# Sixteen projection tiles of the third layer: one product of 512 columns and one of 256 in place of three of 256

## The reference, cut to what matters

```python
h = rmsnorm(x, norm_mix_g)
proj = h @ w_in                 # query, key, value of an mLSTM; output gate; query, key, value of a
                                # dilated attention (1536 columns each); gates (2048)
q, k = q_a / sqrt(64), k_a      # 3 groups x 8 heads x 64
y_b = dilated attention(q, k, v_a)
y_a = mLSTM(...)
merged = sigmoid(g_a) * (y_a @ w_proj_a) + sigmoid(g_b) * (y_b @ w_proj_b)
x = x + merged @ w_out
```

## Time and profile before

| | |
|---|---|
| median of 3 runs | 1105.75 us |
| profiled execution | 1105.73 us |
| its span | 1103.6 us |
| TensorE busy | 1090.9 us, 99% |
| VectorE busy | 757.8 us, 69% |
| ScalarE busy | 600.3 us, 54% |
| GpSimd busy | 149.6 us, 14% |

### The profile page before, as it was taken

The page is one execution under the profiler, slowest core; times in us unless marked ns, Lnnn a source line. Parts: engine busy times, 40 slices in busy tenths (PEclk is TensorE's granted clock), DMA queues, the critical chain, the costliest instruction groups (busy, mean ns, idle before and its releaser), DMA issues.

```text
span 1103.6 us, 17798 instructions
## 1 busy us (share of the span) xinstructions
PE 1090.9 (99%) x6977; PEld 973.0 (88%) x6977; DVE 757.8 (69%) x1054; ACT 600.3 (54%) x788; POOL 149.6 (14%) x113
## 2 busy tenths in 40 slices
PE   8999999999999999999999999999999999999997
PEld 7868888888998888888889999898899989999997
DVE  6774665656668466656557878576587577988884
ACT  6574644444698464444455546555555357546454
POOL 4652000000377220000030000000000002000003
PEclk9999999999999999999999999999999999999999
DMA  9836565556433156565645654446653556545631
GB/s 303 289 117 123 188 223 191 191 190 233 138 106 129 33 161 217 187 195 189 200 154 191 191 158 144 131 153 231 201 166 121 168 214 229 200 176 196 226 136 39
DMA packets 138929, 194.00 MB, mean 176 GB/s; under 512 B 7163, under 2 KB 113112, under 8 KB 138860
## 3 DMA queue, kind: packets, MB, share of 16 engines
q1 hardware_dynamic: 129004, 184.02, 50.7%
q10 hardware_dynamic: 9248, 8.95, 3.2%
q0 software_dynamic: 608, 0.08, 0.1%
HBM read 191.90 MB, written 6.37 MB: 180 GB/s over the span
## 4 chain that ended last, share of the span: by engine, by line
PE 91%; ACT 4%; DVE 4%; issue 1%; DVEq 0%; ACTq 0%
PE psum L628 22%; PE psum L629 22%; PE psum L630 22%; PE psum L842 11%; PE psum L846 6%; ACT arena L1755 3%; PE psum L716 2%; PE psum L746 1%; PE psum L1392 1%; PE psum L1419 1%; DVE arena L2711 1%; DVE st L2710 1%; PE psum L1353 0%; PE psum L904 0%; PE psum L906 0%
## 5 line engine op out<-in xcount | busy, mean ns | idle before, releaser
L2417 DVE TENSOR_TENSOR wlo<-raw,whi 128x2048 fp32r<-128x2048 f32 (+1 forms) x134 | 302.4, 2264 | 134.8 <-ACT whi L1769 133.7
L1769 ACT ACTIVATE whi<-raw 128x2048 fp32r<-128x2048 f32 (+1 forms) x149 | 277.4, 1871 | 174.0 <-PE psum L630 126.3
L628 PE MATMUL psum<-xA,whi 128*128 128x256 f32 x840 | 239.2, 285 | 0.0
L630 PE MATMUL psum<-xA,wlo 128*128 128x256 f32 x840 | 237.6, 283 | 0.0
L629 PE MATMUL psum<-xA,whi 128*128 128x256 f32 x840 | 237.6, 283 | 0.0
L1726 POOL TENSOR_TENSOR wlo<-raw,whi 128x288 fp32r<-128x288 f32 (+3 forms) x43 | 81.8, 1930 | 746.5 <-ACT whi L1769 746.2
L628 PEld LDWEIGHTS psum<-xA,whi 128*128 128x128 f32 x840 | 160.3, 191 | 2.9 <-DVE wlo L2648 0.9
L629 PEld LDWEIGHTS psum<-xA,whi 128*128 128x128 f32 x840 | 160.4, 191 | 1.1
L630 PEld LDWEIGHTS psum<-xA,wlo 128*128 128x128 f32 x840 | 160.3, 191 | 0.1
L842 PE MATMUL psum<-xA,whi 128*128 128x512 f32 x512 | 122.5, 390 | 0.0
L628 PE MATMUL psum<-whi,xC 128*128 128x512 f32 (+1 forms) x296 | 114.5, 387 | 0.0
(11 more groups left out here) (311 smaller groups left out, 1685.7 us busy)
## 6 DMA issues: line engine op xcount, KB each, us to landing
raw<-in_w_in SPq DMA_DIRECT2D x42, 1024.0 KB, 5.0
raw<-in_mlp_w_up SPq DMA_DIRECT2D x32, 1024.0 KB, 5.3
raw<-in_mlp_w_down SPq DMA_DIRECT2D x32, 1024.0 KB, 4.8
raw<-in_w_gate SPq DMA_DIRECT2D x11, 1024.0 KB, 5.2
raw<-in_w_up SPq DMA_DIRECT2D x11, 1024.0 KB, 6.4
down_raw<-in_w_down SPq DMA_DIRECT2D x6, 1024.0 KB, 8.1
arena<-in_w_down SPq DMA_DIRECT2D x5, 1024.0 KB, 8.3
raw<-in_b_w_o SPq DMA_DIRECT2D x4, 1024.0 KB, 5.0
```

The costliest lines, as they stand in the source:

```text
L628: nc.tensor.matmul(out, lh, rh, start=start, stop=False, skip_group_check=skip)
L630: return nc.tensor.matmul(out, ll, rh, start=False, stop=stop, skip_group_check=skip)
L1769: nc.scalar.activation(whi[split_of[c]][:, 0:n], raw_bufs[raw_of[c]][:, 0:n], ACT.Copy).then_inc(hi_sem, 1)
L2417: V.tensor_tensor(wlo[split_of[c]][:, 0:n], raw_bufs[raw_of[c]][:, 0:n], f(whi[split_of[c]][:, 0:n]), ALU.subtract).then_inc(lo_sem["dve"], 1)
```

## The change

The sixteen tiles qa0 to qa5, ka0 to ka5 and pa0 to pa3 go through a new function `both_parts`. For each half of 128 features it uses a bank of its own: eight products of 512 columns (high weight by both input parts) give the sum with the high inputs in columns 0 to 255 and that with the low inputs in 256 to 511; eight products of 256 columns (low weight) are added to the former. A tile takes two neighbouring banks: qa4 4-5, qa5 6-7, ka0 4-5; qa0 6-7, qa1 4-5, qa2 6-7, qa3 4-5; ka1 6-7, ka2 4-5, ka3 6-7, ka4 4-5, ka5 6-7; pa0 2-3, pa1 4-5, pa2 6-7, pa3 2-3. ScalarE copies columns 256 to 511 of both banks into the tile (`half_copy`), VectorE adds columns 0 to 255 (`parts_added`, two operations), GpSimd multiplies the tile by the row of factors or the gate (`scale_tiles`). TensorE waits for GpSimd's results before the first logits, VectorE before the merge. The diff, without the lines of semaphore plans:

```diff
+            def both_parts(name, x, b):
+                c = index[name]
+                hi, lo = slot(c, KT, 256)
+                weights(c)
+                for nt in range(2):
+                    out = open_bank(f"{name}.{nt}", b + nt)
+                    for k in range(KT):
+                        nc.tensor.matmul(out, hi[:, k, nt * P:nt * P + P], x[:, :, k, :], start=k == 0, stop=False)
+                    for k in range(KT):
+                        ins = nc.tensor.matmul(out[:, 0:SEQ], lo[:, k, nt * P:nt * P + P], x[:, 0, k, :],
+                                               start=False, stop=k == KT - 1)
+                    close_bank(ins, f"{name}.{nt}")
+                chunk_done[c] = full[f"{name}.1"]
...
-            feature_major("qa4", xA, 4)
-            feature_major("qa5", xA, 5)
-            feature_major("ka0", xA, 6)
+            both_parts("qa4", xA, 4)
+            both_parts("qa5", xA, 6)
+            both_parts("ka0", xA, 4)
...
-                feature_major(f"qa{h}", xA, 4 + (h + 3) % 4)
+                both_parts(f"qa{h}", xA, (6, 4)[h % 2])
...
-                feature_major(f"ka{j}", xA, 4 + (j + 2) % 4)
+                both_parts(f"ka{j}", xA, (4, 6)[j % 2])
...
-                wait_read(f"qa{j}.0")
-                wait_read(f"ka{j}.0")
+                pe.wait_ge(*done[f"C.qa{j}"])
+                pe.wait_ge(*done[f"C.ka{j}"])
...
-                feature_major(f"pa{j}", xB, 2 + j % 2)
+                both_parts(f"pa{j}", xB, (2, 4, 6, 2)[j])
...
+            def scale_tiles():
+                pool.wait_ge(*read["C.rs"])
+                run(nc.gpsimd.tensor_scalar(query_row, row_scale, A_DIM ** -0.5, None, ALU.mult))
+                for name in tile_order:
+                    j, row = int(name[2]), query_row if name[0] == "q" else row_scale
+                    for nt in range(2):
+                        pool.wait_ge(*read[f"{name}.{nt}"])
+                    v = C[name[0:2]][:, 2 * j:2 * j + 2, :]
+                    run(T(v, v, row.unsqueeze(1).to_broadcast([P, 2, SEQ]), ALU.mult), done[f"C.{name}"])
+                for j in range(4):
+                    pool.wait_ge(*done[f"C.gate{j // 2}"])
+                    for nt in range(2):
+                        pool.wait_ge(*read[f"pa{j}.{nt}"])
+                    v = C["pa"][:, 2 * j:2 * j + 2, :]
+                    run(T(v, v, C["gate"][:, 2 * j:2 * j + 2, :], ALU.mult), done[f"C.pa{j}"])
...
             split_to("qa0")
             ahead("ka0")
+            def half_copy(name, out):
+                for nt in range(2):
+                    act.wait_ge(*full[f"{name}.{nt}"])
+                b = bank[f"{name}.0"]
+                run(out, psum[:, b:b + 2, SEQ:512], ACT.Copy, done[f"C.{name}.half"])
+            def tile_half(name):
+                half_copy(name, C[name[0:2]][:, 2 * int(name[2]):2 * int(name[2]) + 2, :])
+            for name in ("qa4", "qa5", "ka0"):
+                tile_half(name)
...
                 ahead(f"qa{h}" if h < M_HEADS - 1 else "ka1")
+                tile_half(f"qa{h}")
...
                 ahead(f"ka{j}")
+                tile_half(f"ka{j}")
...
             out_high_c(3)
+            half_copy("pa0", C["pa"][:, 0:2, :])
             split_to("pb1")
+            for j in range(1, 4):
+                half_copy(f"pa{j}", C["pa"][:, 2 * j:2 * j + 2, :])
             ahead("pb1")
...
+            def parts_added(name, out):
+                dve.wait_ge(*done[f"C.{name}.half"])
+                for nt in range(2):
+                    run(V.tensor_tensor(out[:, nt, :], psum[:, bank[f"{name}.{nt}"], 0:SEQ], out[:, nt, :], ALU.add),
+                        read[f"{name}.{nt}"])
             def attention_copy(name):
                 low_ahead(name)
-                dve.wait_ge(*full[f"{name}.0"])
                 j = int(name[2])
...
-                run(ins, read[f"{name}.0"])
+                parts_added(name, C[name[0:2]][:, 2 * j:2 * j + 2, :])
...
                 low_ahead(f"pa{j}")
...
+                parts_added(f"pa{j}", C["pa"][:, 2 * j:2 * j + 2, :])
...
+                dve.wait_ge(*done[f"C.pa{k}"])
                 run(V.tensor_tensor(m, m, C["pa"][:, 2 * k:2 * k + 2, :].rearrange("p a b -> p (a b)"), ALU.add),
                     done[f"C.m{k}"])
```

More of the change, by code:

```diff
@@ L433, in program @@
         plan("v_ones_written", ["C.ones"])
+        tile_order = ["qa4", "qa5", "ka0"] + [f"qa{j}" for j in range(4)] + [f"ka{j}" for j in range(1, 6)]
+        plan("dilated_tile_half", [f"C.{n}.half" for n in tile_order + [f"pa{j}" for j in range(4)]])
+        plan("dilated_tile_scaled", [f"C.{n}" for n in tile_order])
+        plan("projected_gated", [f"C.pa{j}" for j in range(4)])
         plan("output_gate_ready", ["C.so"])
@@ L515, in program @@
              "pa": area(0, KT, SEQ), "m": area(2048, 2, 2 * SEQ)}
+        query_row = area(19848, SEQ)
         neg_row = area(16904 + 2 * SEQ, SEQ + P, rows=M_HEADS)
@@ L1696, in scale_queries @@
                         done[f"A.qn{j}"] if blk else None)
+            def scale_tiles():
[13 more added lines that the diff above has]
+                    run(T(v, v, C["gate"][:, 2 * j:2 * j + 2, :], ALU.mult), done[f"C.pa{j}"])
             for c in range(NC):
+                if chunks[c]["name"] == "ffn.g0":
+                    scale_tiles()
                 if chunks[c]["name"] in ("wo0", "wo1"):
```

## The result

The changed kernel takes **1120.76 us** (median of 4 runs, 1119.7 to 1121.72) against 1105.87 (1105.38 to 1107.28) for the kernel before: ratio 1.0132, 95% interval 1.0115 to 1.015. It is slower by 14.9 us; 10.3 were forecast. The profiled execution took 1121.72 us, its span is 1119.9.

What follows compares the result with a forecast made beforehand. TensorE, busy 99% of the span, was taken to bound the kernel. From 1105.75 us the terms +9.1 - 0.9 - 1.1 + 0.5 + 0.7 = +8.3, with the clock +10.3, gave 1116.0 us, range 1112.5 to 1120.5.

Steps and rivals of the forecast that it cites:

- The likeliest case: Whole kernel: ka0 waits for VectorE's adds behind ScalarE's late copy of qa4; 1116.0 us, own range 1114.5 to 1118, 59%.
- rival (b): Ka and merge stages: more waits, or low clock for all of ka0; terms 1.5, 1.5, 3.5 us; 1119.5 us, 16%.
- The first reuse: At ka0, wanting bank 4 again: TensorE idles 7.75 us for qa4's copy and adds; +9.1 us including three tiles' gains.
- The clock behind the hole: At ka0, after the long idle time: granted clock starts at its lower level; +2.0 us, bounds nothing and 5.5.
- Rival (a): At ka0: the clock doesn't fall, or rises at once; 1114.0 us, 18%.
- The tile's price: Each of the sixteen tiles: 5.54 us on TensorE, 0.22 us less than 5.76; 3.5 us in all.
- The ka tiles: Five tiles ka1 to ka5: gain of 1.1 us, and +0.5 us because bank 6 comes free late for ka3.
- The merge: Behind the pa tiles: weights arrive late, m0's low ready at 893.45 where TensorE wants it at 892.15; +1.3 us.
- GpSimd beside VectorE: Where both engines overlap: only GpSimd's operations lengthen, VectorE isn't slowed; no term in the sum.
- rival (c): Before ka0: qa4's copy done before bank 4 is wanted, decided at about 676.9; matmuls' gain remains, 1102.2 us, 5%.

Runs made afterwards that it cites:

- experiment 1: Changed kernel with ScalarE's copy of qa4 moved before the two sigmoids and that of qa5 before the splits of qa0 and qa1; 1112.34 us.
- experiment 2: Changed kernel with only bank pairs changed (qa5 2-3, ka0 6-7, later tiles following), no engine's order; 1119.12 us.
- experiment 3: Changed kernel with 33 unused products of 512 columns filling the wait in front of ka0; 1117.3 us.
- experiment 8: Changed kernel with three bank pairs at the start, qa0 split before the last silu, qa4's and qa5's copies right behind it, pa1's copy between pb0's and pb1's splits; 1105.43 us.
- Experiment 4: Changed kernel with ScalarE's copy of pa1 moved between the splits of pb0 and pb1, instead of behind both; 1115.68 us.
- experiment 6: Changed kernel with GpSimd's multiplications cut to one column each, all waits kept; 1120.25 us.
- experiment 9: Kernel of experiment 8 with the exponential moved before the split of qa1 and the sigmoids; 1104.08 us.
- experiment 7: Changed kernel with the reorderings of experiment 1 and Experiment 4 together (copies of qa4, qa5 and pa1 earlier on ScalarE); 1108.03 us.
- experiment 10: Kernel of experiment 8 with three unused products of 512 columns in front of C.cols; 1103.85 us.
- experiment 5: Changed kernel with ten unused products of 512 columns filling the wait before co0; 1120.49 us.

## Why the prediction was right, and where it was short

The likeliest case held in sign and mechanism: ka0 waited for VectorE, VectorE for ScalarE's copy, and that stood behind the split of qa1. The time, 1120.76, lies 4.8 above the forecast and 0.3 above the range's upper end; on which side of that end it falls is luck, since the four runs spread from 1119.7 to 1121.72. In number it is nearer to rival (b), more waits and more low clock; three fifths of the 4.4 us by which the steps of the table exceed their forecast (14.7 against 10.3) are of its kind, at a place that it had only in part.

- **The first reuse.** Forecast a hole of 7.75 us, the copy at 685.3; measured 7.49, and 687.00 under a shift of 1.82, thus 685.2. That ScalarE's order made it, and not the reused pair, is shown by experiments 1 and 2. The step, with the tiles' gain and the clock, is 11.55 us where 9.1 + 2.0 stood.
- **The clock behind the hole.** Forecast +2.0; experiment 3 gives 2.3. With the rule cited there (the Trainium skill, "TensorE: Matmul & The Clock Gate", section "Why this matters for your kernels") the traces agree for this hole: 0.50 behind it, 1.00 where it was filled. Rival (a) is out. The price is not fixed: the same hole in experiment 2, in front of small products, cost 4.1 us.
- **The tile's price, mis-sized.** 5.54 us and -0.22 a tile; measured 5.58 where tiles stand back to back, and 2.2 us for all sixteen by experiment 8, 0.14 each, so -3.5 should have been -2.2. The pace of 0.226 came from 16 products in a row; here groups of eight alternate, and eight take 1.84 us, 0.230 each.
- **The ka tiles.** Of the +0.5 for a late ka1 0.34 us came, before ka3, ended by line 3041 as said. The gain was 0.1 us a tile (28.98 against 28.49 for five), not 0.22.
- **The merge, the step that failed in size.** The mechanism was as written, raw buffer, landing, split, low; +1.3 was the sum with 5.0 us for the landing. The first chunk came 6.1 us behind the low that freed its buffer, so the wait was 2.0 and the step 2.23. The upper bound of 2.2 had been taken from just such a row.
- **A second fall of the clock,** +1.71, was in no case. The sum asked about the clock once, at the long hole, and treated a wait of about a microsecond and a half as costing itself alone. With the 0.9 of the wait it is most of what is missing. Experiment 4 removes both at once, and behind the wait of 0.77 us in experiment 3 the clock did not fall. Neither did it behind the 2.09 us of experiment 2, so the length of the wait alone would not have told; the term could have had a chance and a price of its own.
- **GpSimd beside VectorE, wrong.** I concluded from rows 12 that only GpSimd pays. It was one overlap, and in it VectorE's low had begun first (24.77 against 26.04); where GpSimd's operation was there first, VectorE paid. The rule that I set aside (the Trainium skill, "Advanced Engine Details and Errata", section "GPSIMD Details") is borne out by experiment 6: 3.27 against 2.29. That the sum needed no term for it was luck: VectorE's time was off the path there, and in experiment 9 it is not.
- **The other side, rival (c).** It named one condition, qa4's copy done before bank 4 is wanted. That was too little: with the copy early (experiment 1) 1112.3 us remain, and with pa1's copy moved too (experiment 7) 1108.0, still above the kernel before. The time falls clearly below it only when the waits for banks 7 and 4 and the one before C.cols are gone as well (experiments 9 and 10), and then to 1104, since the tiles' gain is two thirds of what (c) had. Its 676.9 is off too: by the prediction's own rows qa5 cannot end before 678.7 while it waits for bank 7.

What stays open: why products of 512 columns in groups of eight cost 0.004 us more each, why 0.38 us of idle time in experiment 8 bring the clock down while 1.8 and 0.8 us in experiment 1 do not, and why 2.00 us before co0 bring it down in the changed kernel and 2.09 in experiment 2 do not. The small products behind the 0.38 us are a candidate, but the kernel before and experiments 9 and 10 have the same ones without a fall.

## What to carry to other kernels

When an operation is divided among more engines, the price of its parts matters less than their place in each queue: find for every new reader of a bank what stands in front of it, and put the copy that frees a resource ahead of work that only prepares. Ask of each new wait, the short ones too, whether TensorE's clock survives it, and what comes next on the chain of buffer, landing and split. A gain of 2 us in 1100 was there, but it showed in the median only when the last wait of 0.38 us was gone.

## What the runs showed of the hardware

- The granted clock fell to 0.50 at four waits: 7.49 us before ka0 (its price 2.3 us), 7.55 us before C.cols in experiment 2 (4.1 us), 2.00 us before co0 (1.7 us), and 0.38 us before C.cols in experiment 8, where it averaged 0.54 in 685 to 687 (1.6 us). It stayed at 1.00 at 1.80 and 0.82 us with 3.1 us of products between them (experiment 1), at 0.77 us before co0 (experiment 3), and at 2.09 us before co0 (experiment 2). So the length of a wait alone did not decide it here.
- Where a wait was filled with unused products the clock stayed at 1.00: 2.3, 1.6 and about 1.6 us came back in experiments 3, 5 and 10. In the second case experiment 2 shows the same without filling.
- VectorE and GpSimd, both with operands in SBUF: the operation that began later was the longer one. Beginning inside a GpSimd operation, 128x2048 on VectorE took 3.27 us instead of 2.29; beginning 0.14 us behind one of VectorE's, 128x512 on GpSimd took 2.24 instead of 1.29. Three gating operations of GpSimd beside VectorE's lows took 7.98 us, and the low of 891.33 that had begun first kept its 2.29.
